# Two attention mixers planned with durations of their own, and a GpSimd split that waits for VectorE's

## The chip, the cores and the metric

One core of one Trainium2 chip runs the whole program. The metric is the device time in microseconds (us) of one execution; less is better. Engine names: PE is TensorE (its weight loads are shown as PEld), DVE is VectorE, ACT is ScalarE, POOL is GpSimd, SP is SyncE, whose queue issues the weight loads from HBM.

## What is computed

A decoder trunk of two layers on 256 tokens of width 1024, all in float32. Cut to what matters:

```
layer 0 (A): qkv = x @ a_w_qkv;  16 heads of 64, causal softmax attention over the one block of 256
             x = LN(alpha*x + o @ a_w_o)
layer 1 (B): q = x @ b_w_q;  kv = x @ w_kv_shared;  8 heads, each  softmax(q1 k1) - lam*softmax(q2 k2)  times v
             o = o * rsqrt(mean(o^2) + eps) * g * (1 - lambda_init);   x = LN(alpha*x + o @ b_w_o)
both:        up, gate = split(x @ w_in);  up = causal conv of width 3 over tokens + bias
             x = LN(alpha*x + (gelu(up) * gate) @ w_out)
```

q and k are rotated in a quarter of each head's width. Float32 accuracy is reached by splitting each operand of a large product into a high and a low part (`w_hi`, `w_lo`, both float32r), and three matmuls for one product: hi by hi, hi by lo, lo by hi.

## The kernel before

**Weights.** All weights come in 98 chunks of 1 MB (`CHUNK` = 2048 columns of 128 partitions), 49 for each layer: 12 chunks of qkv weights (two for each of six column groups, `cg` 0 to 5), 4 of the output projection (`wo`), 33 of the FFN. Chunk c lands in raw slot c % 3. ACT copies it to `w_hi[c % 4]` (the step `split_hi`, line 670), then DVE computes `w_lo = raw - w_hi` (`split_lo`, line 867), and PE may use it. In a mixer both steps are done in halves of 128x1024. A raw slot is loaded anew when `lo_done` says that its chunk is split; a `w_hi` slot is written anew when `chunk_used` says that PE is through with it. So a split that is late delays PE directly and the transfer three chunks on.

**The mixer's work.** PE has a fixed list of products: `proj` (cg, kt, st), 96 of them, eight to a chunk, and then 32 `wo` products. Between these it does attention's steps: `scores` (lines 1256, 1259), `probT` transposes (1267), `pv` (1285 and 1290 in A, 1300 to 1302 in B), and in B `outT` (1308). ACT drains PSUM (`drain`, 717), takes the `exp` (741), copies `probT_out` (751), `pv_out` (756, the tile `head_rows`), `out_hi` (766, 769). DVE does `rope` (968 to 977), `turn` (986: sixteen transposes of 32x32 blocks for each of q and k, in two steps of eight; both must be through before the first `scores`), `mask` (996), `norm`, `subln` (1038), `out_lo` (1044, 1047). Their orders are fixed when the program is built.

**The planner.** `mixer_schedule(layer, first_chunk)` plays the mixer through once for each layer. `STEPS` gives each kind its engine and its duration; `after` its dependencies. `HOP` is added when a dependency crosses engines, `LANDING` is the time from a freed raw slot to the data of the next chunk. At each turn the planner takes the step that can start first on its engine; where several could start at the same time, the one with the smallest ready time plus the kind's `PATIENCE` (0 where none is given):

```
start = max(r, free[engine])
key = (start, engine == "PE" and -1.0, r + PATIENCE.get(kind, 0.0))
```

So a positive patience puts a kind behind the others, a negative one ahead of them. PE, ACT and DVE then issue their steps in the planned order and wait on semaphores for what really happens: a plan that is wrong in time shows as an engine that stands in front of a step whose data are late while a later step could run.

**The end of a mixer.** The last 20 or so wo products run without anything between them. Meanwhile ACT and DVE split the first FFN chunk (c = first chunk + 16) and ACT takes the high part of the next (c + 1); the low part of c + 1 is GpSimd's, in two halves: the first as soon as ACT's high part is there, the second after the layer norm of the first 128 tokens (`POOL_SPLITS`, `pool_split_lo`, line 623). DVE then adds the residual (903), takes statistics (893), normalizes (908 to 924), and PE transposes the result (1176) as the input of the FFN. Two of the 32 wo products (6, 1, 1 and 7, 1, 1) stand behind the first of these transposes.

Of the kernel before, what the change touches and what calls it, by code (L numbers as in the profile page):

```python
# [45 lines left out]
def two_pi_pieces():  # L46
# [12 lines left out]
STEPS = {  # L59
    "proj": ("PE", 0.65),  # L60
    "drain": ("ACT", 0.5),
    "rope": ("DVE", 1.7),
    "qkT": ("PE", 0.43),
    "turn": ("DVE", 2.8),
    "qkT_out": ("ACT", 0.48),
    "scores": ("PE", 1.7),
    "mask": ("DVE", 0.6),
# [16 lines left out]
PV_GROUPS = ((0, 1, 2, 3), (4, 5, 6, 7), (8, 9, 10, 11), (12, 13), (14, 15))  # L84
PAIR_GROUP = [n for n, heads in enumerate(PV_GROUPS) for _ in heads[::2]]
TURN_FILLS = ("qkT", "probT", "outT")
LANDING, FIRST_LANDING = 4.8, {3: 9.5, 4: 12.5, 5: 15.5}
HOP = 0.2

PATIENCE = {"split_hi": 7.0, "split_lo": 5.0, "drain": 1.0, "rope": 2.0, "turn": 2.0, "out_hi": -1.5, "out_lo": -1.0}  # L90


def mixer_schedule(layer, first_chunk):
# [8 lines left out]
    after = {}  # L102
# [23 lines left out]
    for step in products:  # L126
        c = chunk(*step[1:3]) if step[0] == "proj" else first_chunk + 12 + step[1] // 2
# [7 lines left out]
    for step in products:  # L135
        c = chunk(*step[1:3]) if step[0] == "proj" else first_chunk + 12 + step[1] // 2
# [27 lines left out]
    for m in range(16):  # L164
# [11 lines left out]
        if A and m % 2 and m in [heads[-1] for heads in PV_GROUPS]:  # L176
            n = PAIR_GROUP[m // 2]
# [30 lines left out]
    end = {}  # L208
    turn_bank_free = 0.0
# [3 lines left out]
    def ready(step):  # L213
        times = [0.0]
        for n in after[step]:
            if n not in end:
                return None
            times.append(end[n] + (0.0 if STEPS[n[0]][0] == STEPS[step[0]][0] else HOP))
            if step[0] == "subln" and n[0] == "mean":
                times[-1] += 0.9  # L220
        if step[0] == "split_hi" and step[2] == 0:
            freed = ("split_lo", step[1] - RAW_RING, 1)
            if freed in after and freed not in end:
                return None
            times.append(end[freed] + LANDING if freed in after else FIRST_LANDING.get(step[1], 0.0))
        if step[0] in TURN_FILLS:
            if turn_bank_free is None:
                return None
            times.append(turn_bank_free + HOP)
        return max(times)  # L230

    while products_left or any(waiting.values()):
        best = None
        for kind, steps in waiting.items():
            if steps and (r := ready(steps[0])) is not None:
                engine = STEPS[kind][0]
                start = max(r, free[engine])
                key = (start, engine == "PE" and -1.0, r + PATIENCE.get(kind, 0.0))
                if best is None or key < best[0]:
                    best = (key, steps[0], start)  # L240
        if products_left and (r := ready(products_left[0])) is not None:
            start = max(r, free["PE"])
            key = (start, 1.0, r)
            if best is None or key < best[0]:
                best = (key, products_left[0], start)
        _, step, start = best
        engine, takes = STEPS[step[0]]
        if step[0] == "norm" and not A:
            takes = 1.1
        if A and step[0] in ("pv", "out_hi", "out_lo") and len(PV_GROUPS[step[1]]) == 4:  # L250
            takes = {"pv": 1.65, "out_hi": 0.5, "out_lo": 0.62}[step[0]]
        elif A and step[0] == "pv":
            takes = 1.0
        (products_left if step[0] in ("proj", "wo") else waiting[step[0]]).pop(0)
        free[engine] = end[step] = start + takes
        order[engine].append(step)
        if step[0] in TURN_FILLS:
            turn_bank_free = None
        elif step[0] in ("qkT_out", "probT_out") or not A and step[0] == "out_lo":
            turn_bank_free = end[step]  # L260
# [3 lines left out]
def yoco_trunk(nc, x, positions, a_w_qkv, a_w_o, w_kv_shared, b_w_q, b_w_o, b_lambda, b_subln_g,  # L264
# [19 lines left out]
    for layer in range(LAYERS):  # L284
        c = layer * LAYER_CHUNKS + QKV_CHUNKS + WO_CHUNKS
        POOL_SPLITS[2 * layer, 0] = ([(c + 1, 0)], [(c + 1, 1)])
        c = (layer + 1) * LAYER_CHUNKS
# [12 lines left out]
    def by_vector(c):  # L300

        return (c, 1) not in POOL_PARTS

    schedule = [mixer_schedule(layer, layer * LAYER_CHUNKS) for layer in range(LAYERS)]

    fills = [(layer,) + step for layer in range(LAYERS) for step in schedule[layer]["PE"]
# [42 lines left out]
    with ExitStack() as ctx:  # L349
# [3 lines left out]
        def sem(name):  # L353
            return ctx.enter_context(nc.semaphore(name))
# [80 lines left out]
        hi_done, lo_done, chunk_used = sem("hi_done"), sem("lo_done"), sem("chunk_used")  # L435
# [129 lines left out]
        def _(pool):  # L565
# [50 lines left out]
            def pool_split_lo(c, half):  # L616

                if half == 0 and c in BY_HALVES:
                    pool.wait_ge(half_hi_done, BY_HALVES.index(c) + 1)
                else:  # L620
                    pool.wait_ge(hi_done, c + 1)
                part = slice(half * CHUNK // 2, (half + 1) * CHUNK // 2)
                nc.gpsimd.tensor_tensor(w_lo[c % RING][:, part], raw[c % RAW_RING][:, part],  # L623
                                        w_hi[c % RING][:, part].bitcast(F32), ALU.subtract).then_inc(pool_lo_done, 1)

            pool.wait_ge(lo_done, FIRST)
            for n in range(2 * LAYERS):
                if n % 2 == 0:
                    pool.wait_ge(*((norm_x_done, 4 * n) if n else (proj_drained, 6)))
                    for tile, src in ((gain, ln_g), (shift, ln_b)):  # L630
                        pool.dma_start(tile[:, :, :], bass.AP(tensor=src.tensor, offset=src.offset + n * D,
                                                              ap=[[0, P], [D, 2], [1, D]])).then_inc(norm_in, 16)
                if n == 2:
                    for p in range(MAPS // 2):
                        pool.wait_ge(mean_sq_done, p + 1)
                        nc.gpsimd.tensor_tensor(rms_inv[:, p % 2, :], mean_sq[:, p % 2, :], minus_half[:, :],
                                                ALU.pow).then_inc(rms_done, 1)
                for st in range(ST):
                    before, after = POOL_SPLITS.get((n, st), ((), ()))
                    for c, half in before:  # L640
                        pool_split_lo(c, half)
                    pool.wait_ge(var_done, ST * n + st + 1)
                    nc.gpsimd.tensor_tensor(std_inv[:, st:st + 1], var_eps[:, st:st + 1], minus_half[:, 0:1],
                                            ALU.pow).then_inc(std_done, 1)
                    if (n, st) == (2 * LAYERS - 1, 0):
                        for half in range(2):
                            cols = slice(half * HALF, (half + 1) * HALF)
                            pool.wait_ge(scaled_done, half + 1)
                            nc.gpsimd.tensor_tensor(xs[:, 0, cols], xs[:, 0, cols], shift[:, n % 2, cols],
                                                    ALU.add).then_inc(norm_x_done, 1)  # L650
                    for c, half in after:
                        pool.wait_ge(norm_x_done, 4 * n + 2 * st + 2)
                        pool_split_lo(c, half)
# [816 lines left out]
```

## Time and profile before

| | us |
|---|---|
| median of 3 runs | 615.63 (615.22 to 618.59) |
| profiled execution | 615.26 |
| its span, first to last instruction | 613.5 |
| PE busy in the span | 598.8 (98%) |
| PE weight load busy | 506.9 (83%) |
| DVE busy | 478.3 (78%) |
| ACT busy | 331.8 (54%) |
| POOL busy | 56.5 (9%) |

The mixer of layer A lies at about 7 to 120 us, its FFN up to 306, the mixer of layer B at 306 to 419, its FFN up to 606, and the last layer norm behind that. Starts in the rows are from the span's start. Matmuls overlap: a 512-column matmul is shown with some 0.39 us and the next one starts 0.227 us after it.

### The profile page before, as it was taken

The numbers are of one execution on the slowest core, as the hardware profiler recorded it, in microseconds if no ns is written. First come the engines' busy times: TensorE is split into PE (matmuls) and PEld (weight loads), VectorE is DVE, ScalarE is ACT, GpSimd is POOL, SyncE is SP. The second block draws the span as 40 slices with busy tenths as digits, with TensorE's granted clock in tenths as the row PEclk, the third lists the DMA queues.
The fourth block names the chain that finished last, engine by engine and source line by source line (L and its number), as shares of the span: only waits on it lengthen the run. The fifth ranks groups of instructions, "written<-read, shape, count | busy, mean of one in ns | idle before, by whom it ended". The sixth has DMA issues, their size and how long they took to land.

```text
span 613.5 us, 8717 instructions
## 1 busy us (share of the span) xinstructions
PE 598.8 (98%) x3284; PEld 506.9 (83%) x3284; DVE 478.3 (78%) x865; ACT 331.8 (54%) x540; POOL 56.5 (9%) x79
## 2 busy tenths in 40 slices
PE   8999999999999999999999999999999999999995
PEld 6887777798888888889888788788988888888894
DVE  4899974876778887777679997868777777777756
ACT  5657875446444445455435587953655555444530
POOL 5200000300000000000520013022000000000002
PEclk9999999999999999999999999999999999999998
DMA  8768542254566665554535565223835555555501
GB/s 304 259 238 310 202 142 70 70 191 153 206 206 206 205 205 195 189 190 185 204 148 196 205 207 188 89 70 136 275 109 183 192 204 202 188 190 183 198 2 68
DMA packets 69238, 109.84 MB, mean 179 GB/s; under 512 B 2332, under 2 KB 47692, under 8 KB 68684
## 3 DMA queue, kind: packets, MB, share of 16 engines
q1 hardware_dynamic: 68332, 105.09, 50.0%
q0 software_dynamic: 576, 4.19, 1.7%
q8 instruction: 26, 0.43, 0.3%
q14 instruction: 16, 0.13, 0.1%
q10 hardware_dynamic: 288, 0.00, 0.0%
HBM read 108.23 MB, written 1.05 MB: 178 GB/s over the span
## 4 chain that ended last, share of the span: by engine, by line
PE 83%; DVE 13%; ACT 2%; issue 1%; DVEq 0%; ACTq 0%
PE wide L1163 13%; PE wide L1165 13%; PE wide L1164 13%; PE score L1365 11%; PE score L1368 6%; PE outb L1365 5%; PE turn L1365 5%; DVE w_lo L867 5%; PE turn L1368 3%; PE outb L1368 3%; DVE qT L986 2%; DVE kT L986 2%; PE turn L1267 1%; ACT w_hi L670 1%; PE score L1176 1%
## 5 line engine op out<-in xcount | busy, mean ns | idle before, releaser
L867 DVE TENSOR_TENSOR w_lo<-raw,w_hi 128x2048 fp32r<-128x2048 f32 (+1 forms) x118 | 213.0, 1827 | 61.6 <-ACT w_hi L670 61.4
L670 ACT ACTIVATE w_hi<-raw 128x2048 fp32r<-128x2048 f32 (+1 forms) x126 | 181.9, 1483 | 33.7 <-PE wide L1165 14.3
L1163 PE MATMUL wide<-w_hi,xT 128*128 128x512 f32 (+1 forms) x256 | 96.6, 377 | 0.5 <-DVE w_lo L933 0.5
L1163 PE MATMUL wide<-w_hi,oT_hi 128*128 128x512 f32 x240 | 95.3, 397 | 0.2 <-DVE oT_lo L1110 0.2
L1164 PE MATMUL wide<-w_lo,oT_hi 128*128 128x512 f32 x240 | 93.7, 391 | 0.0
L1165 PE MATMUL wide<-w_hi,oT_lo 128*128 128x512 f32 x240 | 93.5, 390 | 0.0
L1165 PE MATMUL wide<-w_hi,xT 128*128 128x512 f32 (+1 forms) x256 | 93.2, 364 | 0.0
L1164 PE MATMUL wide<-w_lo,xT 128*128 128x512 f32 (+1 forms) x256 | 93.0, 363 | 0.0
L1365 PE MATMUL score<-xT,w_hi 128*128 128x512 f32 x288 | 71.9, 391 | 0.0
L798 ACT ACTIVATE qT<-kT,conv_cols 128x256 f32<-128x256 f32 x36 | 21.7, 602 | 87.8 <-DVE kT L1076 87.8
L1365 PEld LDWEIGHTS score<-xT,w_hi 128*128 128x128 f32 x288 | 52.8, 188 | 10.1
L1163 PEld LDWEIGHTS wide<-w_hi,xT 128*128 128x128 f32 x256 | 48.3, 189 | 10.4 <-issue 2.5
L1165 PEld LDWEIGHTS wide<-w_hi,xT 128*128 128x128 f32 x256 | 48.3, 189 | 7.8
L1164 PEld LDWEIGHTS wide<-w_lo,xT 128*128 128x128 f32 x256 | 48.4, 189 | 6.5
L1165 PEld LDWEIGHTS wide<-w_hi,oT_lo 128*128 128x128 f32 x240 | 45.1, 188 | 9.7
L1163 PEld LDWEIGHTS wide<-w_hi,oT_hi 128*128 128x128 f32 x240 | 45.2, 188 | 9.3 <-issue 0.9
L1164 PEld LDWEIGHTS wide<-w_lo,oT_hi 128*128 128x128 f32 x240 | 45.2, 188 | 8.1
L623 POOL TENSOR_TENSOR w_lo<-raw,w_hi 128x1024 fp32r<-128x1024 f32 x8 | 20.2, 2535 | 246.5 <-ACT w_hi L670 242.9
L819 ACT ACTIVATE oT_hi<-qT 128x256 fp32r<-128x256 f32 x44 | 16.8, 417 | 46.0 <-DVE qT L1105 43.0
L1368 PEld LDWEIGHTS score<-xT,w_lo 128*128 128x128 f32 x288 | 39.3, 190 | 2.8
L1368 PE MATMUL score<-xT,w_lo 128*128 128x256 f32 x288 | 40.1, 282 | 0.0
L1085 DVE SCALAR_TENSOR_TENSOR qT<-kT,conv_cols,qT 128x255 f32<-128x255 f32 x36 | 17.4, 484 | 24.2 <-ACT qT L798 24.2
(182 smaller groups left out, 870.0 us busy)
## 6 DMA issues: line engine op xcount, KB each, us to landing
raw<-in_ffn_w_in SPq DMA_DIRECT2D x44, 1024.0 KB, 5.1
raw<-in_ffn_w_out SPq DMA_DIRECT2D x22, 1024.0 KB, 4.9
raw<-in_a_w_qkv SPq DMA_DIRECT2D x9, 1024.0 KB, 5.5
raw<-in_w_kv_shared SPq DMA_DIRECT2D x8, 1024.0 KB, 5.2
raw<-in_a_w_o SPq DMA_DIRECT2D x4, 1024.0 KB, 5.0
raw<-in_b_w_q SPq DMA_DIRECT2D x4, 1024.0 KB, 6.0
raw<-in_b_w_o SPq DMA_DIRECT2D x4, 1024.0 KB, 4.9
raw<-in_a_w_qkv SPq DMA_DIRECT2D x4, 512.0 KB, 8.3
```

The costliest lines, as they stand in the source:

```text
L623: nc.gpsimd.tensor_tensor(w_lo[c % RING][:, part], raw[c % RAW_RING][:, part], w_hi[c % RING][:, part].bitcast(F32), ALU.subtract).then_in ...
L670: ins = nc.scalar.activation(w_hi[c % RING][:, part], raw[c % RAW_RING][:, part], ACT.Copy)
L798: nc.scalar.activation(conv[:, tt, :], up_of(peeled, tt), ACT.Identity, scale=conv_cols[:, layer, bass.ds(2 * FT + 2 * i + tt, 1)], bias=c ...
L819: nc.scalar.activation(into[:, tt, :], hidden[:, tt, :], ACT.Copy).then_inc(hhi_done, 1)
L867: ins = nc.vector.tensor_tensor(w_lo[c % RING][:, part], raw[c % RAW_RING][:, part], w_hi[c % RING][:, part].bitcast(F32), ALU.subtract)
L986: last = nc.vector.transpose(turned[:, :, :, 32 * i:32 * i + 32], tokens[:, :, :, 32 * b:32 * b + 32])
L1085: link(nc.vector.scalar_tensor_tensor(conv[:, tt, 1:SEQ], up[:, 0:SEQ - 1], conv_cols[:, layer, bass.ds(FT + 2 * i + tt, 1)], conv[:, tt, ...
L1163: nc.tensor.matmul(dst, a_hi, b_hi, start=start, stop=False, skip_group_check=True)
L1164: nc.tensor.matmul(dst, a_hi, b_lo, start=False, stop=False, skip_group_check=True)
L1165: return nc.tensor.matmul(dst, a_lo, b_hi, start=False, stop=stop, skip_group_check=True)
L1365: nc.tensor.matmul(parts, w_hi[slot][:, tile_cols[kt]], xT[:, :, kt, :], start=kt == 0, stop=False, skip_group_check=True)
L1368: last = nc.tensor.matmul(parts[:, 1, :], w_lo[slot][:, tile_cols[kt]], xT_hi[:, kt, :], start=False, stop=kt == KT - 1, skip_group_check= ...
```

## The change

Three things change. The planner's `LANDING`, `HOP` and `PATIENCE` become tuples, one entry for each layer, with other values. A new table `TAKES` overrides the durations of `STEPS` by layer. And in GpSimd's program, for even n (the layer norm behind each mixer), GpSimd waits for `lo_done` of c before its first half of the split of chunk c (that is, until DVE has split the chunk ahead). No arithmetic changes, and the products stay in their order.

```diff
-LANDING, FIRST_LANDING = 4.8, {3: 9.5, 4: 12.5, 5: 15.5}
-HOP = 0.2
-
-PATIENCE = {"split_hi": 7.0, "split_lo": 5.0, "drain": 1.0, "rope": 2.0, "turn": 2.0, "out_hi": -1.5, "out_lo": -1.0}
+LANDING, FIRST_LANDING = (5.8, 5.7), {3: 9.5, 4: 12.5, 5: 15.5}
+HOP = (0.3, 0.22)
+
+PATIENCE = (
+    {"split_hi": 3.0, "split_lo": 4.0, "drain": 2.5, "rope": 6.0, "turn": 4.0, "out_hi": -1.5, "out_lo": -1.0,
+     "exp": 23.5, "mask": 2.5, "probT_out": -12.0},
+    {"split_hi": 16.5, "split_lo": 3.5, "drain": 1.0, "rope": 4.0, "turn": -5.0, "out_hi": -1.5, "out_lo": -1.0,
+     "pv_out": 21.0, "exp": 16.0, "subln": -11.5, "mask": -1.5},
+)
+TAKES = (
+    {"proj": 0.66, "rope": 1.89, "qkT": 0.46, "turn": 2.95, "qkT_out": 0.67, "scores": 1.56, "exp": 0.81, "norm": 0.68,
+     "probT": 0.39, "split_hi": 0.89},
+    {"proj": 0.683, "rope": 1.41, "qkT": 0.29, "turn": 4.62, "scores": 1.67, "pv": 0.68, "pv_out": 0.37, "square": 0.66,
+     "subln": 0.49, "outT": 0.27, "out_hi": 0.46, "wo": 0.72, "split_hi": 0.94, "split_lo": 1.09},
+)
...
-                key = (start, engine == "PE" and -1.0, r + PATIENCE.get(kind, 0.0))
+                key = (start, engine == "PE" and -1.0, r + PATIENCE[layer].get(kind, 0.0))
...
         engine, takes = STEPS[step[0]]
+        takes = TAKES[layer].get(step[0], takes)
...
                     for c, half in before:
+                        if n % 2 == 0:
+                            pool.wait_ge(lo_done, c)
                         pool_split_lo(c, half)
```

`HOP` and `LANDING` are read as `HOP[layer]` and `LANDING[layer]` where they were plain numbers.

## Rows read from the trace of the kernel before

**Rows 1.** The page's chain that ended last, shares of the span by engine.

```profile
PE 83%; DVE 13%; ACT 2%; issue 1%; DVEq 0%; ACTq 0%
```

**Rows 2.** Waits of PE over the span: us in total, times, longest.

```profile
PE score L1176 <- DVE xs L924: 2.1, 2, 1.1
...
PE outb L1300 <- ACT head_rows L756: 1.0, 1, 1.0
PE outb L1247 <- DVE kT L986: 0.9, 1, 0.9
PE score L1256 <- DVE kT L986: 0.9, 1, 0.9
```

**Rows 3.** Stretches: start, end, length, PE busy (instructions), clock, DMA share, GB/s.

```profile
20.00:107.00 87.00, 85.97 (x478) 1.00 0.56 198
322.00:406.00 84.00, 81.89 (x444) 1.00 0.50 174
```

**Rows 4.** Timeline: PE's last product before the first scores of each layer (start, length).

```profile
46.32 0.39 PE L1165 MATMUL wide<-w_hi,xT 128*128 128x512 f32 x1
...
348.08 0.39 PE L1165 MATMUL wide<-w_hi,xT 128*128 128x512 f32 x1
```

**Rows 5.** Timeline of DVE and ACT before the first scores.

```profile
20.44 3.89 ACT L670 ACTIVATE w_hi<-raw 128x1024 fp32r<-128x1024 f32 x4
...
24.75 3.57 DVE L986 STREAM_TRANSPOSE qT<-q_rows 32x256 f32<-32x256 f32 x8
...
38.12 2.36 DVE L867 TENSOR_TENSOR w_lo<-raw,w_hi 128x1024 fp32r<-128x1024 f32 x2
40.39 7.19 DVE L986 STREAM_TRANSPOSE kT<-k_rows 32x256 f32<-32x256 f32 x16
...
342.13 7.19 DVE L986 STREAM_TRANSPOSE kT<-k_rows 32x256 f32<-32x256 f32 x16
```

**Rows 6.** Timeline of the end of mixer A: PE, DVE, POOL.

```profile
109.00 4.57 DVE L867 TENSOR_TENSOR w_lo<-raw,w_hi 128x1024 fp32r<-128x1024 f32 x2 [2.81 <-ACT w_hi L670]
110.00 2.48 POOL L623 TENSOR_TENSOR w_lo<-raw,w_hi 128x1024 fp32r<-128x1024 f32 x1 [65.44 <-ACT w_hi L670]
...
111.91 0.39 PE L1165 MATMUL wide<-w_hi,oT_lo 128*128 128x512 f32 x1
113.49 0.67 DVE L903 SCALAR_TENSOR_TENSOR xs<-xs,wide 128x512 f32<-128x512 f32 x1
...
114.81 0.67 DVE L903 SCALAR_TENSOR_TENSOR xs<-xs,wide 128x512 f32<-128x512 f32 x1
116.72 1.02 POOL L643 TENSOR_TENSOR std_inv<-var_eps,minus_half 128x1 f32<-128x1 f32 x1 [4.24 <-DVE var_eps L909]
...
117.35 0.39 PE L1165 MATMUL wide<-w_hi,oT_lo 128*128 128x512 f32 x1
118.81 1.32 PE L1176 MATMUL score<-ident,xs 128*128 128x128 f32 x8 [1.07 <-DVE xs L924]
```

**Rows 7.** The same at the end of mixer B: DVE, POOL.

```profile
408.36 4.56 DVE L867 TENSOR_TENSOR w_lo<-raw,w_hi 128x1024 fp32r<-128x1024 f32 x2 [1.80 <-ACT w_hi L670]
409.36 2.49 POOL L623 TENSOR_TENSOR w_lo<-raw,w_hi 128x1024 fp32r<-128x1024 f32 x1 [6.32 <-ACT w_hi L670]
```

**Rows 8.** Timeline of POOL's second half and DVE beside it, mixer A.

```profile
119.33 0.68 DVE L903 SCALAR_TENSOR_TENSOR xs<-xs,wide 128x512 f32<-128x512 f32 x1
119.49 2.42 POOL L623 TENSOR_TENSOR w_lo<-raw,w_hi 128x1024 fp32r<-128x1024 f32 x1 [1.76 <-DVE xs L924]
```

**Rows 9.** Timeline of ACT and PE where PE waits for `head_rows`, mixer B.

```profile
393.08 0.51 ACT L741 ACTIVATE probs<-masked,neg_max 128x256 f32<-128x256 f32 x1
...
394.45 0.46 PE L1300 MATMUL outb<-v_rows,probsT 128*128 128x128 f32 x2 [1.03 <-ACT head_rows L756]
394.94 1.99 ACT L670 ACTIVATE w_hi<-raw 128x1024 fp32r<-128x1024 f32 x2
```

**Rows 10.** A stretch of mixer B: busy PE, PEld, DVE, ACT, POOL, as rows 3.

```profile
382.00:406.00 24.00, 22.79 (x132) 18.44 (x131) 17.89 (x69) 19.36 (x66) 2.76 (x4) 1.00 0.38 123
```

More of the change, by code:

```diff
@@ L217, in ready @@
                 return None
-            times.append(end[n] + (0.0 if STEPS[n[0]][0] == STEPS[step[0]][0] else HOP))
+            times.append(end[n] + (0.0 if STEPS[n[0]][0] == STEPS[step[0]][0] else HOP[layer]))
             if step[0] == "subln" and n[0] == "mean":
@@ L224, in ready @@
                 return None
-            times.append(end[freed] + LANDING if freed in after else FIRST_LANDING.get(step[1], 0.0))
+            times.append(end[freed] + LANDING[layer] if freed in after else FIRST_LANDING.get(step[1], 0.0))
         if step[0] in TURN_FILLS:
@@ L228, in ready @@
                 return None
-            times.append(turn_bank_free + HOP)
+            times.append(turn_bank_free + HOP[layer])
         return max(times)
```

## The prediction

> **What bounds the kernel now.** I read the page first: PE is busy for 98% of the span, and the chain that ended last is 83% PE [rows 1]. PE is the bound, so the time is PE's work plus the moments in which it stands still. Neither part of the change touches PE's work: same instructions, same shapes, clock already full [rows 3]. What can move is idle time. PE's own waits name it: twice the transposes behind a mixer wait for DVE's normalization, 2.1 us together; twice the first scores of a layer wait for DVE's transposes of k, 0.9 and 0.9; once PV waits for ACT's copy of `head_rows`, 1.0 [rows 2]. The stretches agree: in 20 to 107 us PE is idle 87.00 - 85.97 = 1.03, in 322 to 406 it is 84.00 - 81.89 = 2.11 [rows 3], and the rest is at the mixers' ends. Together the visible idle time which this change could reach is 2.1 + 1.03 + 2.11 = 5.2 us. That is the ceiling, apart from some 0.1 us wherever PE goes over from one kind of step to another, which no plan removes altogether.
>
> **GpSimd's wait.** At the end of mixer A, DVE splits chunk c in two halves from 109.00, 4.57 us. An undisturbed pair takes 2.36 at 38.12, or 2.27 to the next start [rows 5]. The difference, 2.2 to 2.3 us, is nearly GpSimd's 2.48 us of the same kind of operation, which begins at 110.00 inside it. Layer B repeats it: 4.56 us, with GpSimd's 2.49 starting a microsecond in [rows 6, 7]. So DVE stood while GpSimd ran. Beside GpSimd's other half at 119.49, DVE's residual addition (one operand in PSUM) took its usual 0.68 [rows 8].
>
> The Trainium skill, "SBUF — State Buffer", section "Who interferes with whom", says the same as an exclusive lock: a DVE instruction with two SBUF inputs contends with a GpSimd one that reads SBUF, one with at most one SBUF input does not. By that rule the moved half, too, would cost the residual addition nothing; a lock that held every DVE instruction would hand the 2.4 us straight back, which is rival 2 below.
>
> With the wait, DVE's pair ends at 109.00 + 2.27 = 111.3. GpSimd starts there and ends at about 113.8; what is queued behind it on GpSimd is std_inv, which starts at 116.72 after 4.24 us of waiting for var_eps [rows 6] and will be asked for at 115.6: free in time. PE wants GpSimd's chunk only in the FFN, behind the transposes of 118.8 and more products: covered by some 9 us. What DVE does next is then set by PE: the last matmul of the first output bank starts at 111.91 and lasts 0.39, so 112.3, against 113.49 for the addition now [rows 6]. The second bank is through six matmuls later, 6 x 0.227 = 1.36, so at 113.66, against 114.81 for the second addition now. So the whole chain of normalization moves by 1.1 us. The transposes could start at 118.81 - 1.1 = 117.7; PE comes free at 117.35 + 0.23 = 117.58 [rows 6]. 1.07 of idle time shrinks to 0.1. Layer B has the same durations [rows 7] and, of the 2.1 us, the other 1.0 [rows 2]. **Term 1: -2.0 us** (bounds: 0 if DVE is stopped elsewhere, -2.2). What is late next is PE itself, so nothing more comes of it. SP's reload of chunk c's slot goes out 2.3 us earlier, one transfer of those that SP issues anyway, at a DMA share that is 0.5 on average [rows 3].
>
> **The plan up to the first scores.** I worked the planner's rule through with the new numbers. Why A waits now is plain: a `turn` is planned with 2.8 us and takes 3.6 (eight transposes, 3.57 at 24.75; sixteen, 7.19 at 40.39 [rows 5]), so k's transposes end later than planned while PE, at its planned place, has done 55 proj products.
>
> Layer A, new: patience 3 for `split_hi` against 2.5 for `drain`, and 4 for `split_lo` against 6 for `rope`, put chunk 3's split ahead of the drains and the rope; then, for DVE, rope, chunk 4, turn, chunk 5, turn, chunk 6, rope, chunk 7, turn, turn, chunk 8. That is one chunk more ahead of the k transposes than now: 2.27 us. Their end moves from 47.58 to 49.9, or to 51.2 if chunk 3 can't be split on ACT before 20.44 and DVE waits for it first [rows 5]. In the plan, turns end at 41.6 and PE takes seven more products ahead of `scores`. A product is 3 x 0.227 = 0.68, so PE comes there at 46.55 + 4.77 = 51.3 instead of 46.55 [rows 4]. 51.3 is later than either: the wait of 0.9 goes. Chunks 4 to 7 are each ready before PE, by this order at 27.2, 33.0, 38.9 and 42.7 against needs at 30.9, 36.3, 41.8 and 47.2 (eight products to a chunk, counted back from 46.55).
>
> Layer B, new: turn's patience of -5 puts all k transposes ahead of chunk 56, and its duration of 4.62 (too long by 1.0) lets PE finish chunk 55 before `scores`. DVE: without that chunk's pair (2.27) ahead of them the transposes end at 349.32 - 2.27 = 347.05 [rows 5]. PE: one product fewer, so at 348.08 + 0.23 - 0.68 = 347.63 [rows 4]. No wait; chunk 56 is split by 349.3, and PE, through with the scores, wants it at 349.4: just in time. **Term 2: -1.8 us** (bounds: 0 if my order is off by a product or two on either side; -1.8).
>
> **The plan behind that.** Some 200 steps a layer follow, which I can't work out, and no row shows the new order. What the rows give are bounds. Gain: what is left of layer B's 2.11 without the 0.9, 1.2 [rows 2, 3]. Loss: a step placed too early costs what its producer is late, by the waits here about 1 us at a time, and one or two such are usual. The new durations are nearer to the trace for some kinds (proj 0.683 for 0.68, turn 2.95 for 3.6 in A) and further for others (turn in B, `split_hi` 0.89 in A for 3.89 / 4 [rows 5]). B's attention starts 1.5 us sooner, A's 2.3 to 4 later with DVE having slack behind it. The patience of `pv_out`, 21, works against the 1.0, that of `subln`, -11.5, for it. **Term 3: 0** (bounds -1.2 and +2 or more), taken in the middle because rows point both ways.
>
> **Sum.** -2.0 - 1.8 + 0 = -3.8 us, against the profiled execution's 615.26 (span 613.5 and 1.76 around it): 611.5. The median of runs lies 0.37 above: 611.8.
>
> **Rivals.** What a measurement of this kernel can tell from no change is about 0.5%, 3.1 us; so "faster" begins at 612.55.
>
> 1. Forecast: terms 1 and 2 hold, the rest of the plan costs at most 0.7 or gains: 609.9 to 612.5. Chance 0.60.
> 2. GpSimd's wait gives nothing, because its half, now at 111.3 to 113.8, holds up the additions at 112.3 instead. For: two overlapping pairs on record. Against: the addition at 119.33 kept 0.68 [rows 8]. It would take back all of term 1: 613.8. Chance 0.07.
> 3. New waits in the later plan, two or three of 1 us: PE runs ahead of attention because more chunks are split first, has used up its proj products and stands before a `wo` or `pv`. For: that is just what the gap before 394.45 is, where ACT was still at `exp` at 393.08 [rows 9]. Against: in A, eight wo products lie between the last PV and the first that needs it. With 1 to 3.8 us lost: 612.6 to 615.6. Chance 0.25.
> 4. Slower, by one mechanism: `pv_out` with patience 21 always comes last on ACT. PV of head k waits for `pv_out` of k-1, so each of heads 4 to 7 may stand behind a `split_hi` pair of 1.99 us [rows 9], when PE has no product to put in its place. One such costs 2, two undo the forecast (615.6), and it takes four, 7.6 us, for 0.5% slower: 619. Exps and drains share this fate, so it needs ACT to be full where it is busy 19.36 of 24 us now [rows 10]. Chance 0.08.
>
> Faster 0.60; within 0.5% 0.32, from rivals 2 and 3; slower 0.08. The range runs from 610.0, the ceiling of 5.2 and a few transitions off 615.6, to 614.6, which holds rival 2 and most of 3: about 0.13 left out above, 0.05 below. The forecast's own range is 609.9 to 612.5.
>
> **What would show each step.** Term 1: DVE's pair at both mixer ends 2.3 us instead of 4.57, GpSimd's half starting after it, the additions still 0.68, and PE's wait for the normalized xs below 0.2. Term 2: no wait of PE for `kT`. Term 3: the list of PE's waits between the first scores and 107, and 406. It would be wrong if PE's idle time in these two stretches were above the 3.1 us of now, or if a chunk's split came late to PE, which would be a wait for `w_lo`, of which mixers have none today.

## The result and the profile after

| | before | after |
|---|---|---|
| median, us | 617.11 (615.22 to 621.02, 4 runs) | 609.08 (608.82 to 609.34, 4 runs) |
| profiled execution | 615.26 | 608.82 |
| its span | 613.5 | 607.0 |

The ratio is 0.988 with the interval 0.9854 to 0.9906: faster by 1.2%. The prediction said 611.8, in a range of 610.0 to 614.6; the time lies 0.9 us below its low end. Profile against profile the gain is 6.44 us, where the sum said 3.8. The rest of the gain between the medians is that executions of the kernel before scatter over 6 us and those of the kernel after over half of one, which the experiments come back to. (The diff adds 14 lines ahead of the functions concerned, so line 867 is 881 after, 903 is 917, 924 is 938, 1176 is 1190; GpSimd's 623 is 635.)

PE's waits in the profile after, over the whole span (us in total, times, longest), beside [rows 2]:

```profile
PE wide L1198 <- DVE zeros L941: 1.5, 1, 1.5
PE wide L1177 <- DVE w_lo L947: 0.4, 2, 0.2
PE turn L1190 <- DMA xs<-in_x: 0.3, 1, 0.3
PE wide L1177 <- DVE w_lo L881: 0.3, 1, 0.3
PE wide L1177 <- DVE oT_lo L1124: 0.2, 1, 0.2
```

All four lines of [rows 2] are gone. The 1.5 for `zeros` is the last layer norm, outside the change; the 0.4 for `w_lo`, L947, are two small waits at the start of mixer A, which the kernel before has too (0.26 and 0.21). New is 0.3 for `w_lo`, L881. The stretches, with the columns of [rows 10]:

```profile
20.00:107.00 87.00, 87.00 (x487) 69.35 (x486) 72.16 (x208) 60.02 (x132) 1.33 (x2) 1.00 0.57 197
322.00:406.00 84.00, 83.58 (x454) 68.30 (x453) 73.28 (x225) 62.75 (x162) 6.91 (x9) 1.00 0.45 158
```

PE has no idle time left in A's stretch (1.03 before) and 0.42 in B's (2.11 before). DVE around the end of mixer A, beside [rows 6] and [rows 8]:

```profile
106.76 2.36 DVE L881 TENSOR_TENSOR w_lo<-raw,w_hi 128x1024 fp32r<-128x1024 f32 x2 [2.81 <-ACT w_hi L684]
110.12 0.69 DVE L917 SCALAR_TENSOR_TENSOR xs<-xs,wide 128x512 f32<-128x512 f32 x1 [1.00 <-PE wide L1179]
111.48 0.69 DVE L917 SCALAR_TENSOR_TENSOR xs<-xs,wide 128x512 f32<-128x512 f32 x1
```

DVE's pair takes 2.36 (4.57 before); its additions wait for PE now and keep 0.69, although GpSimd's half lies beside them, and GpSimd is free for `std_inv` in time:

```profile
109.20 2.42 POOL L635 TENSOR_TENSOR w_lo<-raw,w_hi 128x1024 fp32r<-128x1024 f32 x1 [65.17 <-DVE w_lo L881]
113.41 1.02 POOL L657 TENSOR_TENSOR std_inv<-var_eps,minus_half 128x1 f32<-128x1 f32 x1 [1.79 <-DVE var_eps L923]
```

At the end of mixer B, beside [rows 7], the two halves of DVE's split no longer follow each other directly, but each has its undisturbed length:

```profile
402.72 1.23 DVE L881 TENSOR_TENSOR w_lo<-raw,w_hi 128x1024 fp32r<-128x1024 f32 x1 [1.80 <-ACT w_hi L684]
...
404.26 1.21 DVE L881 TENSOR_TENSOR w_lo<-raw,w_hi 128x1024 fp32r<-128x1024 f32 x1
...
405.55 2.40 POOL L635 TENSOR_TENSOR w_lo<-raw,w_hi 128x1024 fp32r<-128x1024 f32 x1 [6.53 <-DVE w_lo L881]
```

In mixer A, PE goes from its last product straight into the transposes, 0.37 after that product's start where it was 1.46 in [rows 6]:

```profile
115.13 0.39 PE L1179 MATMUL wide<-w_hi,oT_lo 128*128 128x512 f32 x1
115.50 1.21 PE L1190 MATMUL score<-ident,xs 128*128 128x128 f32 x7
```

The first transposes behind a mixer start at 118.81 and 418.17 before, at 115.50 and 411.73 after. Counted from PE's first product of each mixer (7.34 and 306.04 before, 7.03 and 302.73 after), mixer A became 3.0 us shorter and mixer B 3.1. The two FFNs between and behind them kept their length within 0.1. The remaining 0.3 lies before the first product, whose start varies from 6.98 to 7.76 between the profiles of all kernels here and isn't the change's.

The start of the scores, beside [rows 4] and [rows 5]; PE in both layers and DVE's transposes ahead of them:

```profile
50.55 0.39 PE L1179 MATMUL wide<-w_hi,xT 128*128 128x512 f32 x1
50.78 0.32 PE L1261 MATMUL outb<-ident,conv_rows 88*128 88x88 f32 x2
...
344.11 0.39 PE L1179 MATMUL wide<-w_hi,xT 128*128 128x512 f32 x1
344.42 0.49 PE L1270 MATMUL score<-kT,qT 64*128 64x128 f32 x4
...
346.32 0.50 PE L1177 MATMUL wide<-w_hi,xT 128*128 128x512 f32 x1 [0.32 <-DVE w_lo L881]
```

```profile
45.63 4.06 DVE L1000 STREAM_TRANSPOSE kT<-k_rows 32x256 f32<-32x256 f32 x9
...
336.67 7.20 DVE L1000 STREAM_TRANSPOSE kT<-k_rows 32x256 f32<-32x256 f32 x16
343.91 3.50 DVE L881 TENSOR_TENSOR w_lo<-raw,w_hi 128x1024 fp32r<-128x1024 f32 x3
```

A (add 0.31, by which the mixer's first product starts sooner than before): transposes through at 49.69 + 0.31 = 50.00, forecast 49.9; PE there at 50.78 + 0.31 = 51.09, forecast 51.3. B (add 3.31, the same shift there): 343.87 + 3.31 = 347.18, forecast 347.05; PE 344.34 + 3.31 = 347.65, forecast 347.63.

### The profile page after: what moved, and what is told of

Its sections match the earlier page's. It is cut to its first block, busy times and chain, and to the rows that moved or that the text cites. A ratio compares the mean times of both kernels' runs of the same rounds, so it can differ in the third digit from the quotient of the medians.

```text
span 607.0 us, 8719 instructions
## 1 busy us (share of the span) xinstructions
PE 597.1 (98%) x3284; PEld 506.6 (83%) x3284; DVE 474.0 (78%) x865; ACT 331.8 (55%) x540; POOL 52.4 (9%) x79
## 4 chain that ended last, share of the span: by engine, by line
PE 93%; DVE 6%; issue 1%; ACT 0%; DVEq 0%; ACTq 0%
PE wide L1177 16%; PE wide L1179 16%; PE wide L1178 16%; PE score L1379 11%; PE score L1382 6%; PE outb L1379 5%; PE turn L1379 5%; PE turn L1382 3%; PE outb L1382 3%; DVE w_lo L881 2%; PE turn L1281 1%; DVE qT L1000 1%; DVE kT L1000 1%; PE score L1190 1%; PE outb L1299 1%; PE score L1179 1%
## 5 line engine op out<-in xcount | busy, mean ns | idle before, releaser
L881 DVE TENSOR_TENSOR w_lo<-raw,w_hi 128x2048 fp32r<-128x2048 f32 (+1 forms) x118 | 208.7, 1789 | 60.0 <-ACT w_hi L684 59.8
```

What stands on the lines that cost most here:

```text
L881: ins = nc.vector.tensor_tensor(w_lo[c % RING][:, part], raw[c % RAW_RING][:, part], w_hi[c % RING][:, part].bitcast(F32), ALU.subtract)
```

## The experiments

Beside each group of experiments the kernel before ran on the same chip; its fastest executions took 615.09 to 615.30, its medians 615.93 to 616.58. Because it scatters, the ratio of medians mixes two things, and the fastest executions are given beside it. "Down" is this kernel's fastest against 615.1 to 615.3.

### The parts alone

`e1_wait_only`: the kernel before with the wait.

```diff
+                        if n % 2 == 0:
+                            pool.wait_ge(lo_done, c)
                         pool_split_lo(c, half)
```

> The plans of the kernel before, with GpSimd's wait alone. Theory (a mutual hold-up of two operations that both read SBUF twice, and nothing else): DVE's pair at both mixer ends falls from 4.57 to 2.3 us, the transposes behind each mixer start 1.1 to 1.2 us sooner, span 613.5 - 2.3 = 611.2. The waits of PE for kT (0.9, 0.9) and for head_rows (1.0) stay as they are. Rival (the wait only helps together with the new plan, since there ACT splits at other times): less than 1 us.

`e2_plan_only`: the kernel after without these two lines.

> Both new plans, without GpSimd's wait. Theory (terms add): DVE's pair is 4.57 us again, PE waits 1.0 to 1.1 us for the normalized xs at each mixer end, no other wait of PE in the mixers; span 607.0 + 2.3 = 609.3. Rival (the new plan leaves enough room that GpSimd's overlap costs nothing): 607 to 607.5.

`e3_plan_a` and `e4_plan_b`: without the wait, and with the new numbers for one layer alone (e3 for A; e4 the reverse).

```diff
-LANDING, FIRST_LANDING = (5.8, 5.7), ...
-HOP = (0.3, 0.22)
+LANDING, FIRST_LANDING = (5.8, 4.8), ...
+HOP = (0.3, 0.2)
...  PATIENCE[1] as before, TAKES[1] = {}
```

> The new plan in layer A alone, the old one in B, no wait of GpSimd. Theory: the wait of 0.93 for kT in A goes and costs 1.1 with its restart, the late chunk 4 gives 0.25, and some changeovers of PE less: transposes behind mixer A 1.4 to 1.9 us sooner, B unchanged, span 611.6 to 612.1. Rival (the 0.3 us by which the first product came sooner belongs to the plan): the first product at 7.03 rather than 7.34 again.

> The new plan in layer B alone. Theory: PE's waits for kT (0.91) and head_rows (1.03 and 0.17 behind it) go, a wait of 0.3 for w_lo comes: mixer B 2.0 us shorter, span 611.4. Rival (the head_rows wait went because GpSimd's wait or layer A's plan shifted the DMAs): it is there again, 612.6.

| | median (range, runs) | ratio | fastest, down |
|---|---|---|---|
| e1 wait | 616.92 (612.98 to 619.14, 12) | 0.9993 [0.9969, 1.0016] | 2.1 |
| e2 both plans | 611.99 (611.21 to 612.48, 6) | 0.9922 [0.9901, 0.9942] | 3.9 |
| e3 plan A | 613.66 (613.32 to 614.91, 9) | 0.9953 [0.9933, 0.9974] | 1.8 |
| e4 plan B | 614.17 (613.03 to 615.43, 9) | 0.9956 [0.9939, 0.9974] | 2.1 |
| the change | 609.08 (608.82 to 609.34, 4) | 0.988 [0.9854, 0.9906] | 6.3 |

The parts add up: 1.8 + 2.1 = 3.9, the plans together; with the wait's 2.1 it is 6.0 of 6.3. e2 keeps the one wait that the plan can't reach:

```profile
PE score L1188 <- DVE xs L936: 2.1, 2, 1.0
```

But by medians the wait alone gives nothing: its executions lie in two groups, four at 612.98 to 613.96 and seven at 616.73 to 619.14, with one between. Its profile, of 618.13 us, shows where the time goes. GpSimd and DVE between the layers, first before (GpSimd, DVE), then e1:

```profile
298.98 3.26 POOL L623 TENSOR_TENSOR w_lo<-raw,w_hi 128x1024 fp32r<-128x1024 f32 x1 [0.75 <-ACT w_hi L670]
298.77 1.21 DVE L876 TENSOR_TENSOR w_lo<-raw,w_hi 128x1024 fp32r<-128x1024 f32 x1
```

```profile
299.54 2.45 POOL L623 TENSOR_TENSOR w_lo<-raw,w_hi 128x1024 fp32r<-128x1024 f32 x1 [0.43 <-ACT w_hi L672]
299.65 3.41 DVE L878 TENSOR_TENSOR w_lo<-raw,w_hi 128x1024 fp32r<-128x1024 f32 x1
...
307.68 2.81 POOL L623 TENSOR_TENSOR w_lo<-raw,w_hi 128x1024 fp32r<-128x1024 f32 x1 [0.48 <-ACT w_hi L672]
307.50 3.55 DVE L926 SCALAR_TENSOR_TENSOR xs<-xs,std_inv,shift 128x512 f32<-128x512 f32 x2
```

Before, DVE starts its half 0.21 us ahead of GpSimd's and GpSimd is held (3.26). In e1 GpSimd comes 0.11 ahead, and DVE is held (3.41 for 1.21). The layer norm behind it is late, meets GpSimd's next half (3.55 for two that take 1.42 otherwise), and PE waits 1.35 + 0.75 + 0.67. By starts, from the transposes behind mixer A to the first product of mixer B it takes 193.0 us (119.40 to 312.43), and 189.5 in e11 below (117.73 to 307.21): the race costs 3.6. Another 1.5 in this profile is no part of the race: PE's wait for `probsT` that ends at 62, behind weight loads that land late (see the base, below). So the wait's 2.1 us is there, and a race some 190 us later, in code that the change does not touch, takes it back in more than half of the executions. What turns the race was not found.

`e11_wait_and_shared` takes the race away: e1, and GpSimd lets DVE go first there too.

```diff
+                        if (c, half) == (SHARED, 1):
+                            pool.wait_ge(shared_lo_done, 1)
```

> The plans of the kernel before, GpSimd's wait, and a second one: between the layers GpSimd splits its half of the second chunk of layer B only after DVE has split the other half. Theory (the executions over 616 us of the wait alone are those in which GpSimd starts this half 0.1 us before DVE rather than 0.2 us after, so that DVE loses 2.2 us and then, late, meets GpSimd's next half in the normalization): none over 615.6, median 613 to 614.5, where the wait alone had 616.92 and a range of 612.98 to 619.14. Rival (they come from late transfers alone): the range stays as wide.

613.74 (613.03 to 615.23, 9 runs), ratio 0.9957 [0.994, 0.9973]. The upper group is gone, with the fastest executions where e1 has its own:

```profile
299.00 2.40 POOL L623 TENSOR_TENSOR w_lo<-raw,w_hi 128x1024 fp32r<-128x1024 f32 x1 [1.83 <-DVE w_lo L880]
297.70 1.21 DVE L880 TENSOR_TENSOR w_lo<-raw,w_hi 128x1024 fp32r<-128x1024 f32 x1
```

The wait of term 1 is thus worth 2.1 us by itself where that race goes DVE's way. In the profile after, DVE is first again, at 295.46 against GpSimd's 295.67, and none of its four timed executions fell into the upper group.

### Which neighbour GpSimd's half may have

`e10_pool_beside_gain`: the kernel after, with GpSimd's half put later, beside DVE's instructions with two SBUF inputs.

```diff
-                            pool.wait_ge(lo_done, c)
+                            pool.wait_ge(stats_done, 4 * n + 2)
```

> The changed kernel, but GpSimd's first half waits for the second statistics of the first 128 tokens instead of DVE's split: it starts near 112.9 and lies beside the operation that subtracts the mean and multiplies by the gain (both inputs in SBUF). Theory (two operations that each read SBUF, DVE's with two inputs from it, exclude each other, whichever came first): DVE's gain operation grows from 0.7 to about 3 us, PE waits 2 to 3 us for xs at both mixer ends, 613 to 615. Rival (only split beside split collides): the gain operation stays 0.7; GpSimd's std_inv is late by 2 us all the same and PE waits about 1 to 2 us, 611 to 613. The duration of the gain operation tells them apart.

615.87 (612.56 to 620.41, 10), ratio 0.9984 [0.9955, 1.0012]. GpSimd's half, DVE beside it, and PE's wait:

```profile
113.73 2.39 POOL L635 TENSOR_TENSOR w_lo<-raw,w_hi 128x1024 fp32r<-128x1024 f32 x1 [68.95 <-DVE stats L907]
114.00 3.34 DVE L929 SCALAR_TENSOR_TENSOR xs<-xs,moments,gain 128x512 f32<-128x512 f32 x2
...
PE score L1190 <- DVE xs L938: 3.8, 2, 1.9
```

L929 takes 1.41 for its two otherwise, 3.34 here: 1.9 more, and PE's wait at each mixer end is 1.9. The additions of L917, with one input in PSUM, kept 0.69 beside the same half. So what a DVE instruction loses depends on which one the half meets. The length of L929 shows that; PE's 1.9 alone would not, since GpSimd's own `std_inv` stands behind the half, ends at 117.11 and would by itself have held the normalization until 0.2 us before L929 ends at 117.34.

### What the new plan lives on

`e5_durations_only`: the kernel after with the old patience for both layers. `e6_patience_only`: with the old durations, `HOP` and `LANDING`. `e7_measured`: old patience, and durations read from the trace of before.

```diff
e5, e7  PATIENCE: both layers as before
e6      TAKES = ({}, {}), HOP 0.2, LANDING 4.8
e7, e8  TAKES (both layers): "drain": 0.54, "turn": 3.61, "qkT": 0.43, "exp": 0.88, "mask": 0.56,
        "split_hi": 0.96, "split_lo": 1.14, "pv_out": 0.41, ...; HOP 0.1, LANDING 5.4
e8      PATIENCE: as after
```

> The changed kernel with the patience of the kernel before: new durations, HOP and LANDING, GpSimd's wait kept. The plan puts scores behind 56 proj products in A with the old order of DVE, behind 62 in B. Theory (order and durations must go together): A's wait for kT stays, 0.9 - 0.7 = 0.2 or more; B's goes; the head_rows wait depends on the later plan. Fastest runs 609.5 to 612. Rival (durations nearer to the trace are what helps, patience does nothing): as fast as the change, 608.8 to 609.3.

> The changed kernel with the durations, HOP and LANDING of the kernel before: new patience only, GpSimd's wait kept. Scores stand behind 61 proj products in A, k's transposes behind one chunk more, as in the change; in B behind 53 products, where the transposes end at 347 while PE comes at 345.6. Theory: A's wait is gone, B waits 1.4 us for kT; fastest runs 609.5 to 612. Rival (patience is all of it): 608.8 to 609.3.

> The patience of the kernel before with durations as measured in its trace (turn 3.61, rope 1.5, split_hi 0.96, exp 0.88, LANDING 5.4, HOP 0.1 and so on), GpSimd's wait kept. Theory A (PE stands where the plan was wrong in time, so a plan with true times has few waits): no wait of PE over 0.3 us in the mixers, fastest runs 609 to 610. Theory B (the wait for kT and the one for head_rows come from the order, in which attention or the splits lag, and a true plan of a bad order waits as well, only on paper too): waits of 1 us or more stay, 610.5 to 613.

> Measured durations as before, with the patience of the change, GpSimd's wait kept. Theory A: no worse than the change, 608.5 to 609.5. Theory B (each set of patience fits its own durations only): some wait of 0.5 to 2 us appears, 609.5 to 611.5.

| | median (range, runs) | ratio |
|---|---|---|
| e5 | 619.97 (618.42 to 623.9, 12) | 1.0062 [1.004, 1.0084] |
| e6 | 614.88 (614.33 to 618.7, 12) | 0.9966 [0.9947, 0.9986] |
| e7 | 621.06 (620.0 to 624.16, 6) | 1.0073 [1.0048, 1.0099] |
| e8 | 619.55 (617.17 to 622.6, 12) | 1.0043 [1.002, 1.0067] |

All four have the wait, so 613.0, e1's fastest, is what they would take with the old plan. None came out in its expected range; the fastest executions lie 6.4, 2.3, 7.0 and 5.7 us above the ranges' upper ends. The profiles of e5 and e8 also show the race between the layers (DVE's half 3.41 and 3.43), so the fastest executions are the ones to compare. The new durations without the new patience cost 5.4 us, fastest against fastest; the new patience without the durations costs 1.4; the measured durations cost 7.0, and 4.2 with the new patience. Only the pair gives back time. Durations nearer to the trace made the order worse, with PE in front of a late `probsT`:

```profile
PE turn L1280 <- ACT probsT L764: 4.3, 3, 2.4
PE turn L1280 <- DVE oT_lo L1060: 1.4, 1, 1.4
```

The next ones take single entries out of the kernel after. `e14_b_turn_alone` keeps of B's new numbers only what term 2 rests on, `e15_b_no_exp` and `e16_a_no_exp` drop the patience of `exp`, `e9_no_pv_out_subln` those of `pv_out` and `subln`.

```diff
e14  PATIENCE[1] as before but "turn": -5.0;  TAKES[1] = {"turn": 4.62};  HOP, LANDING of B as before
e15  PATIENCE[1] without "exp": 16.0
e16  PATIENCE[0] without "exp": 23.5
e9   PATIENCE[1] without "pv_out": 21.0 and "subln": -11.5
```

> The changed kernel, with layer B's numbers those of the kernel before except turn (patience -5, duration 4.62): k's transposes stand where the change puts them and scores behind 56 products, the rest of B is planned with the old numbers. Theory (B's gain of 2.1 is the opening's: no wait for kT, and attention 2.3 us sooner, which cures the head_rows wait by itself): fastest runs within 0.5 us of the change, 608.8 to 609.4, no wait over 0.4 in 350 to 402. Rival (the later part needs its own numbers): the head_rows wait or a worse one, 610 to 613.

> The changed kernel without exp's patience of 16 in layer B. Theory (ACT must let drains, probT_out and the copies behind pv pass before exps that nobody waits for yet): PE waits 1 to 3 us for ACT's probsT or head_rows between 385 and 402 us, 610 to 612.5. Rival: like the change, 608.8 to 609.4.

> The changed kernel without exp's patience of 23.5 in layer A. Theory: the same on layer A's side; PE waits 1 to 2.5 us for ACT's probsT between 55 and 100 us, 610 to 612. Rival (in A PE has products to spare, so ACT's order doesn't matter): like the change, 608.8 to 609.4.

> The changed kernel with layer B's patience of pv_out (21) and subln (-11.5) left out, both 0. Theory (which of the steps ready at one time goes first decides in the tail of mixer B, where PE has few products left): a wait of PE of 0.5 to 1.5 us returns between 385 and 402 us, fastest runs 609.3 to 610.5. Rival (mixer B's gain comes from exp and split_hi standing back, these two do nothing): 608.8 to 609.3, no such wait. The rival that I put on record as the slower side, pv_out's patience as a cost, would show as faster than the change.

| | median (range, runs) | ratio | above the change, fastest |
|---|---|---|---|
| e14 | 618.95 (617.49 to 624.44, 10) | 1.0041 [1.0011, 1.0072] | 8.7 |
| e15 | 612.8 (612.48 to 614.2, 9) | 0.9935 [0.9912, 0.9957] | 3.7 |
| e16 | 611.2 (611.14 to 611.51, 5) | 0.9911 [0.988, 0.9942] | 2.3 |
| e9 | 609.51 (609.31 to 609.73, 4) | 0.9881 [0.9858, 0.9904] | 0.5 |

PE's waits that came with it, in e14, e15 and e16:

```profile
PE turn L1279 <- DVE oT_lo L1059: 2.8, 1, 2.8
PE wide L1175 <- ACT q_rows L729: 2.5, 1, 2.5
```

```profile
PE turn L1281 <- DVE oT_lo L1061: 1.9, 1, 1.9
PE turn L1322 <- DVE oT_lo L1061: 1.2, 1, 1.2
```

```profile
PE turn L1281 <- DVE probs L1019: 0.9, 1, 0.9
PE wide L1177 <- DVE oT_lo L1058: 0.7, 1, 0.7
```

The early k transposes of layer B, alone, make the kernel slower than before: what they win at the first scores is lost several times over where attention's chain is late, which refutes the theory recorded for e14. In e15 the waits came, but for DVE's `oT_lo` and not for ACT, as had been expected. Putting `exp` behind the splits and drains, which looks like a delay of attention, is what keeps PE fed: 3.7 us in B, 2.3 in A. The one new wait of e9 is 0.4 for `oT_lo`, so `pv_out`'s 21 together with `subln`'s -11.5 does no harm and helps by half a us at most; the two were not tried apart.

### A version without the race

`e13_best`: the kernel after, with e11's two lines, and with GpSimd's loads of gain and shift in layer A at a later drain, so that they don't meet the weight loads around 43 us.

```diff
-                    pool.wait_ge(*((norm_x_done, 4 * n) if n else (proj_drained, 6)))
+                    pool.wait_ge(*((norm_x_done, 4 * n) if n else (proj_drained, 12)))
```

> The changed kernel with the same second wait of GpSimd, and with its loads of gain and shift (1 MB each) in layer A moved from 42.7 us, where they go out within 0.1 us of a weight load, to behind the last drain, some 80 us. Theory: the weight load issued at 43 us takes 5 us in every execution and the order between the layers is fixed, so no execution is slow; in fast ones nothing changes: 608.5 to 609.3, range under 1 us. Rival (the loads at 80 us delay wo or FFN weights): 609.5 to 611.

609.09 (609.07 to 609.77, 4), ratio 0.9877 [0.9854, 0.99]: the change's own 609.08. In the four executions of each there was nothing to win; that doesn't show that a late load or the race would cost the changed kernel nothing.

## Why the prediction was off

**GpSimd's wait, term 1 (-2.0): right, in mechanism and size.** DVE's pair 2.36 (forecast 2.3), additions at 0.69, PE's wait for xs gone, 2.1 us alone in e1's fastest executions. Rival 2 is refuted by the additions after; e10 shows when it would have been true. What the step left out is that a mixer which ends earlier shifts everything behind it, and that a race at the other end of the FFN can go the other way: by medians, the wait alone is worth nothing.

**The plan up to the first scores, term 2 (-1.8): right in mechanism, and in size with one correction each way.** Both waits for `kT` are gone, and the hand-worked times hold to 0.2 us in both layers. Chunk 56, called "just in time", is 0.3 late: the wait at 346.32. (That the mixers had no wait for `w_lo` before was misread: mixer A has two, of 0.26 and 0.21, at its start.)

**The plan behind that, term 3 (0): this is the step that failed.** What is left of the mixers' 6.1 us when terms 1 and 2 are taken off is 2.3: by e3, A gives 1.8 of which the `kT` wait is 1.1, so 0.7; by e4, B gives 2.1 of which `kT` less `w_lo` is 0.7, so 1.4, where the wait for `head_rows` alone was 1.0 [rows 2]. Zero was taken "in the middle because rows point both ways". The rows that pointed towards a loss were of two kinds, and neither held. Nearness of durations to the trace says nothing of the order they make (e7). And the patience of `pv_out`, read as a risk by itself, is harmless beside `subln`'s (e9, and no wait for `head_rows` after); rival 4 asked for four such waits and there is none. One step of the working was not open to the reader of the trace: that `exp` behind everything makes the whole plan fit could have been found only by working it through. Rival 3 is just what e5, e7, e14 show, so its 0.25 stood for a real danger; the change escaped it because its numbers fit each other, those of e9 least of all needed.

**The ceiling (5.2 us): failed too, and with it the low end of 610.0.** It took the idle time that the profile shows as all that could be won. Of that, 4.8 is gone: span less PE's busy time was 613.5 - 598.8 = 14.7 and is 607.0 - 597.1 = 9.9. But the span fell by 6.5; the other 1.7 came out of PE's busy time, for the same 3284 instructions:

```profile
PE 597.1 (98%) x3284; PEld 506.6 (83%) x3284; DVE 474.0 (78%) x865; ACT 331.8 (55%) x540; POOL 52.4 (9%) x79
```

A 512-column matmul is shown with 0.39 us while the next can start 0.227 after it. An instruction that is late by up to 0.16 therefore shows no idle time at all, and a longer wait shows 0.16 too little: the `kT` wait of layer A is 0.93 in the profile of before, but its scores started 1.32 after the last product, at 47.64, against 0.23 after, so 1.09 was won. By starts, the waits that were named gave 2.15 (xs), 1.09 + 0.99 less 0.32 (`kT`, `w_lo`) and about 1.07 (`head_rows`), 5.0 together, of the mixers' 6.1. Of the last 1.1, about 0.3 is B's, where before had one more wait, of 0.17 for `oT_lo` (L1047) behind that for `head_rows`. The other 0.8 is A's, where no further wait that went is listed: what is left by this subtraction can only be delays too short to be shown as anyone's wait. A new plan can reach those, and the ceiling left them out.

**The base.** The sum went from the profiled 615.26 with 0.4 on top; the kernel before scatters up to 621.02 and the kernel after does not. Two sources of scatter show in profiles of other runs, but no slow execution of the kernel before itself was profiled, so their shares in its scatter stay open. One is the race (e1, e5, e8). The other is weight loads that land late: in e4 and e1 the three issued from 50 to 56 us took 6.8 to 7.7 us where they take 5.1 to 5.9 before, and PE waits 1.5 for `probsT` until 62. What makes those late was not found.

## What to carry over

What a better order can win is more than the idle time shown: PE's busy time holds short delays too, so compare starts with the shortest distance at which such instructions follow each other. Where an order is fixed by a planner with fitted numbers, neither how near they are to measured durations nor a single preference tells what the order is worth; the plan has to be worked through to its last step, or its whole effect left open with both signs and a wide range. And a kernel whose engines race for a lock can take back elsewhere what a local repair wins: look for the next place where the two engines start within 0.2 us of each other before trusting the sum.

## What the hardware showed beyond what was expected

**Who starts first.** A DVE instruction with two inputs in SBUF and a GpSimd instruction that reads SBUF exclude each other, whichever was first: 0.1 to 0.2 us at the start decides whether GpSimd loses 0.86 (3.26 for 2.40) or DVE loses 2.2 (3.41 for 1.21). That it is the order of starting, and which operands count, is as the Trainium skill, "SBUF — State Buffer", section "Who interferes with whom", has it. It holds for the two-input steps of the layer norm (L929 in e10, 3.34 for 1.41; L926 in e1, 3.55 for 1.42) as for the subtraction. With one input in SBUF, DVE isn't held: after, the statistics at 117.50 (L907) take their usual 0.69 while GpSimd's half runs from 116.18 to 118.60.

**A long wait costs PE its clock as well.** e14's PE waits 2.5 us at 355 and 2.8 us at 394. The stretches behind, with the columns of [rows 10], show the granted clock, the third number from the end:

```profile
355.50:358.50 3.00, 0.54 (x2) 0.48 (x3) 1.90 (x6) 3.00 (x13) 0.00 (x0) 1.00 0.52 213
358.50:361.50 3.00, 3.00 (x10) 1.97 (x10) 2.83 (x18) 2.96 (x8) 0.00 (x0) 0.59 0.69 191
361.50:364.50 3.00, 3.00 (x23) 2.42 (x22) 2.93 (x16) 0.49 (x1) 0.00 (x0) 0.84 0.39 161
393.00:396.00 3.00, 0.78 (x6) 0.59 (x6) 2.93 (x11) 3.00 (x8) 0.00 (x0) 1.00 0.90 274
396.00:399.00 3.00, 2.45 (x9) 2.19 (x10) 2.72 (x9) 2.12 (x10) 0.13 (x1) 0.60 0.38 109
399.00:402.00 3.00, 2.73 (x17) 2.32 (x17) 0.94 (x4) 1.57 (x7) 0.73 (x2) 0.83 0.96 322
```

After each, the clock is at its lower level, 1.2 GHz, for part of some 6 us. An estimate of the loss from these columns: 3 x 0.41 + 3 x 0.16 = 1.7 us, and 3 x 0.40 + 3 x 0.17 = 1.7. Waits of 5.3 and 3.4 of clock make 8.7 of the 10.3 us by which the span of this profile (617.3) exceeds that of the change (607.0); the other 1.6 was not traced. (e14's fastest execution lies 8.7 above the change; that this is the same figure is chance, since it wasn't the one profiled.) The same 1.7 stands behind the 2.4 in e7, the 2.1 in e5 and e10's 1.9 at the end of mixer A; behind the 1.9 in e15, the 1.8 in e6 and the equal 1.9 at the end of e10's mixer B the clock stayed. In e8 it fell behind two shorter ones, 1.20 and 1.10 close together (to 399.35 and 400.86), and stayed behind a single 1.76 at 89. So the length of one wait doesn't settle it. Before and after have none of it in the mixers, so it is no part of the result; but a rival that counts new waits at their own length, as rival 3 did, is too cheap where a wait of some 2 us, or two of 1 us close together, may cost the clock too.

**A weight load behind a broadcast load.** SP's 1 MB weight load takes 5.2 us when it is issued just ahead of GpSimd's 1 MB load of the gain, as after, and 11.1 just behind it, as in e3 (here after, then e3; the median time to landing stands last):

```profile
raw<-in_a_w_qkv SPq DMA_DIRECT2D x1, 1024.0 KB, 5.2
gain<-in_ln_g POOLq DMA_DIRECT2D x1, 1024.0 KB, 7.6
```

```profile
gain<-in_ln_g POOLq DMA_DIRECT2D x1, 1024.0 KB, 7.0
raw<-in_a_w_qkv SPq DMA_DIRECT2D x1, 1024.0 KB, 11.1
```

The order of the two varies with one and the same plan of layer A: the profiles of e2 and e3 have the weight load behind (11.6 and 11.1), those of after, e9, e10, e14 and e15 have it ahead (5.0 to 5.4). With other plans of A it is behind in e6 and e8 (9.4 and 9.7) and ahead in e16 (5.4). That the late one costs time is likely but not shown alone: the profiled executions of e2 and e3 lie 1.3 and 0.8 above the fastest ones of the same kernels. e13 moved the gain's load away and its weight load took 5.1, as after.
